# Nine 2x2 groups with seven products in the second MLP's down-projection

## The reference

```python
up = causal_dwconv(h @ w_up[l], conv_w[l], conv_b[l])        # 2 x 5632 channels, 3 taps
y = (gelu(up[..., :5632], approximate=True) * up[..., 5632:]) @ w_down[l]   # 5632 -> 2048
x = x + rms_norm_2(y, post_ffn_g[l])
```

## Time and profile before

| | us |
|---|---|
| median of the three runs | 2084.43 |
| the profiled execution | 2085.97 |
| its span, first to last instruction | 2084.2 |
| TensorE busy | 2075.1 |
| VectorE busy | 1332.8 |
| ScalarE busy | 1110.3 |
| GpSimd busy | 117.6 |

### The profile page before, as it was taken

How to read it: one execution, slowest core, us unless ns; L and a number is a source line. 1 busy time by engine, 2 the same in 40 slices (tenths; PEclk the granted TensorE clock), 3 DMA queues, 4 the chain that set the end, 5 groups by cost and what they waited for, 6 DMA issues and landing times.

```text
span 2084.2 us, 23926 instructions
## 1 busy us (share of the span) xinstructions
PE 2075.1 (100%) x9259; PEld 1720.2 (83%) x9259; DVE 1332.8 (64%) x1471; ACT 1110.3 (53%) x1344; POOL 117.6 (6%) x66
## 2 busy tenths in 40 slices
PE   9999999999999999999999999999999999999998
PEld 8888888888888878888888888888888888888887
DVE  6546555666884579666876655566767754576665
ACT  7555554555554455455555544456555534555553
POOL 3000000000000000000002000000111100021110
PEclk9999999999999999999999999999999999999999
DMA  8687666778757776778778777677787766778763
GB/s 294 196 258 230 190 187 222 256 220 260 223 187 223 225 238 210 223 222 232 241 254 242 215 252 229 193 212 233 232 262 223 237 196 192 234 235 257 244 214 120
DMA packets 291906, 469.49 MB, mean 225 GB/s; under 512 B 18512, under 2 KB 82128, under 8 KB 291280
## 3 DMA queue, kind: packets, MB, share of 16 engines
q1 hardware_dynamic: 290928, 463.46, 72.3%
q10 hardware_dynamic: 864, 4.49, 0.6%
HBM read 432.75 MB, written 35.13 MB: 224 GB/s over the span
## 4 chain that ended last, share of the span: by engine, by line
PE 95%; DMA 2%; DVE 1%; ACT 1%; SPq 0%; issue 0%; POOL 0%; ACTq 0%; DVEq 0%; POOLq 0%
PE ps L1714 95%; DMA T<-passed_strip 1%; DMA passed_strip<-T 1%; DVE Wl L1335 0%; SPq L1036 0%; DVE T L1428 0%; ACT Wh L1111 0%; PE ps L1717 0%; ACT hid L1214 0%; ACT T L1171 0%; ACT T L1179 0%; DVE hid L1493 0%; SPq L1057 0%; ACT T L1269 0%; DVE QK L1608 0%
## 5 line engine op out<-in xcount | busy, mean ns | idle before, releaser
L1335 DVE TENSOR_TENSOR Wl<-raw,Wh 128x1024 fp32r<-128x1024 f32 x743 | 921.3, 1259 | 590.5 <-ACT Wh L1111 586.3
L1714 PE MATMUL ps<-Wh,aHL 128*128 128x512 f32 x3712 | 1148.9, 390 | 0.5 <-ACT aHL L1139 0.4
L1111 ACT ACTIVATE Wh<-raw 128x1024 fp32r<-128x1024 f32 x743 | 772.2, 1056 | 585.6 <-PE ps L1714 562.1
L1714 PEld LDWEIGHTS ps<-Wh,aHL 128*128 128x128 f32 x3712 | 697.1, 188 | 146.0 <-issue 1.4
L1714 PE MATMUL ps<-Wl,aHL 128*128 128x512 f32 x1856 | 722.3, 389 | 0.0
L1714 PE MATMUL ps<-Wh,hid 128*128 128x512 f32 x1578 | 489.4, 389 | 1.4 <-DVE Wl L1335 1.4
L1714 PEld LDWEIGHTS ps<-Wl,aHL 128*128 128x128 f32 x1856 | 348.6, 188 | 71.8
L1714 PEld LDWEIGHTS ps<-Wh,hid 128*128 128x128 f32 x1578 | 296.2, 188 | 63.5 <-issue 1.8
L1714 PE MATMUL ps<-Wl,hid 128*128 128x512 f32 x789 | 306.9, 389 | 0.0
L1714 PEld LDWEIGHTS ps<-Wl,hid 128*128 128x128 f32 x789 | 148.1, 188 | 30.6
L1714 PE MATMUL ps<-Wh,oHL 128*128 128x512 f32 x512 | 158.9, 390 | 0.0
(11 more groups left out here) (190 smaller groups left out, 876.4 us busy)
## 6 DMA issues: line engine op xcount, KB each, us to landing
raw<-in_mlp_w_dram SPq DMA_DIRECT2D x256, 512.0 KB, 5.2
raw<-in_w_up_dram SPq DMA_DIRECT2D x176, 512.0 KB, 4.5
raw<-in_sb_w_qkv_dram SPq DMA_DIRECT2D x93, 512.0 KB, 5.3
raw<-in_w_down_dram SPq DMA_DIRECT2D x88, 512.0 KB, 4.4
raw<-in_w_in_dram SPq DMA_DIRECT2D x64, 512.0 KB, 4.9
passed_strip<-T SPq DMA_DIRECT2D x104, 256.0 KB, 4.3
T<-passed_strip SPq DMA_DIRECT2D x208, 128.0 KB, 4.8
raw<-in_sb_w_o_dram SPq DMA_DIRECT2D x32, 512.0 KB, 5.2
```

Source lines behind the costliest of these rows:

```text
L1111: e.activation(Wh[:, i % NW, c], src, ACT.Copy).then_inc(st["hi"][0], 1)
L1335: e.tensor_tensor(Wl[:, i % NW, c], src, Wh[:, i % NW, c].bitcast(F32), ALU.subtract).then_inc(st["lo"][0], 1)
L1714: return e.matmul(o, l, r, start=start, stop=stop, skip_group_check=True)
```

## The change

Three of the four pairs of `w_down_2` get three groups each, from the hidden blocks 0, 1 and 4 of their part; pair 4 stays as it was. The token sums of these blocks are made in the up-projection, after the first and the third gated pair of strips of each part (`MIXED_STRIPS`), from the gate's buffer `E`. The sums of part one go straight into `xn` (`fresh`), and `y_first` adds to it instead of copying.

With A for the plain slabs of a pair's first strip, B for those of its second and G for a group, TensorE's order is now:

- pair 1: A1 to A7, G1, B1 to B3, G2, B4 to B6, G3, B7, A8, A9, B8, B9
- pair 2: A1 to A4, G1, A5 to A7, G2, A8, B1, B2, G3, B3, B4, A9, B5 to B9
- pair 3: A1 to A5, G1, B1, B2, G2, B3, B4, G3, B5, A6, A7, B6, B7

```diff
-    def strip_pair(w, s4, ks, tail, mov, tiles, evacs, koff=0, sevens=(), fold=None):
+    def strip_pair(w, s4, ks, tail, mov, tiles, evacs, koff=0, sevens=(), fold=None, lead=None):
...
-        lead, gap = (4, 3) if tail else (2, 3 if len(plain) > 7 else 2)
-        rest = a[lead:n] + b[:n] if tail else a[lead:n - 1] + b[:2] + a[n - 1:] + b[2:]
+        lead, gap = (lead or 4, 3 if lead is None or len(plain) > 7 else 2) if tail else (lead or 2, 3 if len(plain) > 7 else 2)
+        rest = a[lead:n] + b[:n] if tail else a[lead:n - 1] + b[:lead] + a[n - 1:] + b[lead:]
...
+    MIXED_STRIPS = {0: (0, 2), 8: (2, 1)}
...
                     free["E"] = [lo]
+                    if t0 in MIXED_STRIPS:
+                        free["E"] = [lo, mix_tokens("hid2", "E", *MIXED_STRIPS[t0], [g])]
...
             i = strip_pair("w_down_2", s4, tuple(range(2 * at, 2 * (at + n))), 0 if s4 else 2, "hid2", hid_tiles,
                            [evac_y(c, s4), evac_y(c, s4 + 1)], koff=2 * at)
+                           sevens=(2 * at, 2 * at + 1, 2 * at + 4) if c == 0 or s4 == 0 else (),
+                           fold=fold_into("xn", s4, fresh=c == 0), lead=4 if s4 else 2 * n - 5)
...
-        hid2, = area(("hid2", [128, 24, 2 * TOK], F32R))
+        hid2, hidMix2 = area(("hid2", [128, 24, 2 * TOK], F32R), ("hidMix2", [128, 3, 4, TOK], F32R))
...
+                        if st["fresh"]:
+                            e.tensor_copy(x[:, 0, a], P[:, 0, :]).then_inc(m[1][0], 1)
+                            e.wait_ge(*m[0])
+                            e.tensor_tensor(x[:, 1, a], P[:, 2, :], wsum[:, 0, :], ALU.add).then_inc(m[2][0], 1)
...
+                    elif st["fresh"]:
+                        e.tensor_tensor(x[:, 0, b], P[:, 1, :], wsum[:, 0, :], ALU.subtract).then_inc(m[3][0], 1)
+                        e.wait_ge(*m[2])
+                        e.tensor_tensor(x[:, 1, b], P[:, 1, :], x[:, 1, a], ALU.subtract).then_inc(m[4][0], 1)
...
-                        e.tensor_copy(xn[:, t, cs], ps[st["set"]][:, t, :]).then_inc(st["done"][t][0], 1)
+                        if st["folded"]:
+                            e.tensor_tensor(xn[:, t, cs], xn[:, t, cs], ps[st["set"]][:, t, :], ALU.add).then_inc(st["done"][t][0], 1)
+                        else:
+                            e.tensor_copy(xn[:, t, cs], ps[st["set"]][:, t, :]).then_inc(st["done"][t][0], 1)
```

More of the change, by code:

```diff
@@ L149, in plan_program, with mix_tokens @@
     mixed_tokens = {}
-    def mix_tokens(mov, k, n, need):
+    def mix_tokens(mov, src, k, n, need):
         d = [done("token_mixed") for c in range(4)]
         hi, lo = done("mixed_hi"), done("mixed_lo")
-        step("mix_tokens", mov=mov, k=k, n=n, need=[*need, *free["sums"]], d=d, hi=hi)
+        step("mix_tokens", mov=mov, src=src, k=k, n=n, need=[*need, *free["sums"]], d=d, hi=hi)
         free["sums"] = [lo]
@@ L160, in mix_tokens, with fold_into @@
         return d[3]
-    def fold_into(s4):
+    def fold_into(to, s4, fresh=False):
         def f(sets, k):
             copied = done("fold_copied")
-            marks = [done("folded") for i in range(8)]
-            step("fold", s4=s4, k=k, sums_free=list(free["sums"]), copied=copied, marks=marks)
+            marks = [done("folded") for i in range(5 if fresh else 8)]
+            step("fold", to=to, s4=s4, k=k, sums_free=list(free["sums"]), copied=copied, marks=marks, fresh=fresh)
             def second():
-                step("fold_rest", s4=s4, marks=marks)
+                step("fold_rest", to=to, s4=s4, marks=marks, fresh=fresh)
                 free["sums"], free["set2"] = [marks[-1]], [marks[-1]]
@@ L414, in landed @@
                 if mixed and t0 < 8:
-                    free["T1"] = [lo, mix_tokens("hid1", t0 // 2, 2 if t0 == 0 else 1, [turned])]
+                    free["T1"] = [lo, mix_tokens("hid1", "T1", t0 // 2, 2 if t0 == 0 else 1, [turned])]
                 hid_tiles[t0:t0 + 4] = [lo] * 4
@@ L442, in plan_program @@
             i = strip_pair("mlp_w2", s4, tuple(range(2 * at, 2 * (at + n))), 0 if s4 else 2, "hid1", hid_tiles, evacs, koff=2 * at,
-                           sevens=() if c == 2 and s4 else tuple(range(2 * at, 2 * at + 3)), fold=fold_into(s4))
+                           sevens=() if c == 2 and s4 else tuple(range(2 * at, 2 * at + 3)), fold=fold_into("xN", s4))
             if c == 1 and s4 == 0:
@@ L688, in f @@
                 d = [done("y_kept") for t in range(2)]
-                step("y_first", s4=s4, set=s, mm=k, done=d)
+                step("y_first", s4=s4, set=s, mm=k, folded=st.pop(("fold", s4), None), done=d)
                 free[f"set{s}"] = [d[1]]
@@ L694, in f @@
                 g = done("y_gained") if s4 < 3 else done("y_gained_last")
-                kw = dict(t=t, s4=s4, set=s, mm=k[t], t0_free=list(free["T0"]), y=y, q=q, g=g, g_row=st["g_row"])
+                kw = dict(t=t, s4=s4, set=s, mm=k[t], t0_free=list(free["T0"]), y=y, q=q, g=g, g_row=st["g_row"],
+                          folded=st.get(("fold", s4)))
                 free["T0"] = [q]
@@ L959, in build @@
         square_buf = {"E": E4, "T1": T1[:, :, :], "QK1": mT[:, 8:12, :]}
-        mixes = {"hid1": hidMix1}
+        mixes = {"hid1": hidMix1, "hid2": hidMix2}
         movs = {"aHL": aHL, "oHL1": oHL1, "oHL2": oHL2, "hid1": hid1, "hid2": hid2}
@@ L1348, in vector_program @@
                     d, hi, lo = mixed_rows(st)
-                    src = T1[:, :, :].rearrange("p (k t) q -> p t k q", t=2)
+                    src = (T1[:, :, :] if st["src"] == "T1" else E4).rearrange("p (k t) q -> p t k q", t=2)
                     even, odd = src[:, 0, 0:st["n"], :], src[:, 1, 0:st["n"], :]
@@ L1364, in vector_program @@
                 elif k in ("fold", "fold_rest"):
+                    x = xN if st["to"] == "xN" else xn
                     a, b = [slice((st["s4"] + i) * STRIP, (st["s4"] + i + 1) * STRIP) for i in range(2)]
@@ L1369, in vector_program @@
                         e.tensor_tensor(wsum[:, 0, :], P[:, 0, :], wsum[:, 0, :], ALU.add).then_inc(m[0][0], 1)
[L1370 to L1373, removed]
+                        if st["fresh"]:
[3 more added lines that the diff above has]
+                        else:
+                            e.tensor_tensor(x[:, 0, a], x[:, 0, a], P[:, 0, :], ALU.add).then_inc(m[1][0], 1)
+                            e.wait_ge(*m[0])
+                            e.tensor_tensor(wsum[:, 1, :], P[:, 2, :], wsum[:, 0, :], ALU.add).then_inc(m[2][0], 1)
+                            e.tensor_tensor(wsum[:, 2, :], P[:, 1, :], wsum[:, 0, :], ALU.subtract).then_inc(m[3][0], 1)
+                    elif st["fresh"]:
+                        e.tensor_tensor(x[:, 0, b], P[:, 1, :], wsum[:, 0, :], ALU.subtract).then_inc(m[3][0], 1)
+                        e.wait_ge(*m[2])
+                        e.tensor_tensor(x[:, 1, b], P[:, 1, :], x[:, 1, a], ALU.subtract).then_inc(m[4][0], 1)
                     else:
@@ L1376, in vector_program @@
                         e.tensor_tensor(wsum[:, 0, :], P[:, 1, :], wsum[:, 1, :], ALU.subtract).then_inc(m[4][0], 1)
-                        e.tensor_tensor(xN[:, 1, a], xN[:, 1, a], wsum[:, 1, :], ALU.add).then_inc(m[5][0], 1)
-                        e.tensor_tensor(xN[:, 0, b], xN[:, 0, b], wsum[:, 2, :], ALU.add).then_inc(m[6][0], 1)
+                        e.tensor_tensor(x[:, 1, a], x[:, 1, a], wsum[:, 1, :], ALU.add).then_inc(m[5][0], 1)
+                        e.tensor_tensor(x[:, 0, b], x[:, 0, b], wsum[:, 2, :], ALU.add).then_inc(m[6][0], 1)
                         e.wait_ge(*m[4])
-                        e.tensor_tensor(xN[:, 1, b], xN[:, 1, b], wsum[:, 0, :], ALU.add).then_inc(m[7][0], 1)
+                        e.tensor_tensor(x[:, 1, b], x[:, 1, b], wsum[:, 0, :], ALU.add).then_inc(m[7][0], 1)
                 elif k == "rms":
@@ L1592, in vector_program @@
                 elif k == "y_first":
+                    if st["folded"]:
+                        e.wait_ge(*st["folded"])
                     for t in range(2):
```

2 lines of the change are left out of this document (1 added, 1 removed).

## The result

The changed kernel takes 2092.38 us (median of six runs, 2090.84 to 2093.55), beside 2084.55 us for the kernel before in the same sitting: 1.003 times as long, with a 95% interval of 1.0019 to 1.0041. It is slower, as forecast, by 7.8 us between the medians (0.38%, inside that interval) where the forecast had 5.0. The profiled execution took 2091.95 us, its span is 2089.9.

The account below looks back on a forecast made before the run. TensorE, busy 2075.1 of 2084.2 us, was taken as the bound: 2085.97 - 6.12 + 3.7 (pair 1) + 7.4 (pair 3) = 2091.0, less 1.54 to the median, 2089.4 us. The range leaving out 2 in 10: 2085.5 to 2092.5.

Parts of the forecast that it names:

- What goes: Nine groups take 21 matmuls for 24: 27 x 0.2267 = 6.12 us less on TensorE's path.
- Pair 2 and the token sums at nothing: Pair 2's groups cost nothing; token sums taken as 0, with 0 to 0.5 us for each two-block place.
- Pair 1, 3.7 us: In pair 1, s2 of G2 0.98 us late and B5 2.74 us late, together 3.7 us.
- Pair 3, 7.4 us: In pair 3, s2 0.57, s3 2.40, B3 0.46 and G3's s0 3.96 us late, together 7.4 us.
- Rival 3: The clock falls in pair 3's 3.96 us wait, costing 2.3 us more: 2091.7 us; chance 0.15.
- a granted clock below 1 near pair 3's G3: Listed among the signs that would show the forecast wrong; no size given.
- The gate waits for a break of VectorE: GpSimd's gate product starts only at a break in VectorE's row, then takes 2.26 us.
- The sum: 2085.97 - 6.12 + 3.7 + 7.4 = 2091.0 us, less 1.54 from profiled execution to median: 2089.4 us, 0.24% slower.
- the token sums' 1.54 us until the copy: With two blocks, the token sums cost VectorE 1.54 us until the copy starts, 428.48 to 430.06.
- Rival 2: The splits stay ahead, so only the 6.12 us count: 2078.3 us, faster; chance 0.08.

Follow-up runs that it names:

- pair 2 alone: The changed kernel with the groups of pairs 1 and 3 taken out, token sums still made in all four places: 2082.11 us.
- first filled kernel: The changed kernel with eight zero-weight matmuls run by TensorE in pair 3's wait before s3 of G2: 2091.36 us.
- the second: The changed kernel with eight zero-weight matmuls in pair 3's wait before s3 of G2 and fourteen before s0 of G3: 2092.42 us.
- the kernel with the chain later: The changed kernel with the last up strip's older taps, GpSimd gate product and halves placed later in pairs 1 and 3: 2088.23 us.
- the spread chain: The changed kernel with the last up strip's chain spread over the splits in pairs 1 and 3, and its gate product on VectorE: 2081.14 us.

## Why the prediction was right, and where its terms were off

- *What goes*: 27 matmuls, in pair 2 alone all of its 2.04 us. Right.
- *Pair 2 and the token sums at nothing*: right.
- *Pair 1, 3.7 us*: the two waits together are 1.17 + 2.53 = 3.70. That the sum is met so exactly is luck: the terms were 0.98 and 2.74. What was missing is the slow start behind a wait: the first matmul is 0.34 us before the next in place of 0.2267, and a few after it run a little long, 0.35 in all.
- *Pair 3, 7.4 us*: where the clock did not fall it is 7.57 in the first filled kernel and 8.52 in the second, whose strip landed later. In the profiled execution it was 9.09. Rival 3 came on top of the forecast, and twice: a granted clock below 1 near pair 3's G3, one of the prediction's own signs of being wrong, was there (0.57 from 2007 to 2011). The first fall cost nothing, since it ran out of the wait before s0 of G3 (2.35 us for the forecast's 3.96); the second, behind that wait, cost 1.7 where the rival had 2.3. The prediction had the clock at 0.15 and as one event. In these traces the lower level followed most of the waits of 2.0 to 4.7 us, in pair 1 and in the first MLP too, but not three of them (2.2, 2.4 and 3.8 us).
- *The gate waits for a break of VectorE*: right in every profile here; all gate products of the thirteen profiles, of whatever length, end 2.20 to 2.27 us after the end of VectorE's last instruction before the break. The Trainium skill (SBUF — State Buffer, "SBUF: two separate sides") lets the port pair that VectorE and GpSimd share go to whichever of their instructions starts first. The runs agree that the other one then stands for the whole of it (2.77 us for the fourth sum), but between VectorE's back-to-back instructions GpSimd never came first.
- *The sum*: taking off the 1.54 us between the profiled execution and the median was sound. Most of that distance was the wait of 1.4 us in the first MLP, a chance of one execution, and the kernel before came out at 2084.55 again. The forecast had the change at 4.98 us, and the medians differ by 7.83. Of the missing 2.85 us, 1.7 lie in pair 3, by the clock, and 0.35 in pair 1, by the slow starts. The remaining 0.8 are in no pair: 0.43 is that the profiled execution lies so much below its own median, and no trace places the rest. The median ended 0.1 us inside the upper end of the range, 2092.5.
- *A slip without weight*: the token sums' 1.54 us until the copy is 1.58 by the starts given for it, 428.48 and 430.06.
- *Rival 2 (the splits stay ahead)* named the place that decides, and the spread chain shows it: with the taps out of the way of the splits and the gate product in VectorE's own row, pair 1 has no wait at all.

## What to carry to other kernels

Work that is placed by a count of pieces moves in time when the pieces get shorter: look for what stands between the splits of the new pieces before counting the matmuls saved. GpSimd's product beside a busy VectorE cost twice here, first by waiting for a hole and then by making VectorE stand for its length; on this critical chain the same operation in VectorE's own row was cheaper (1.14 us for some 2.1). And where VectorE has no lead left, as in pair 3, the saved matmuls came back as waits (54.34 us with the groups and the chain spread, 54.40 without groups): such groups can be left out.

## What the runs showed that was not expected

- A hole of 0.12 us in VectorE's row, where an instruction waits for the result of the one before, was enough for GpSimd to get in, in both pairs of the kernel with the chain later: 2.08 and 2.03 us for VectorE.
- TensorE's granted clock went to 0.50 behind a wait of 2.4 us in one execution and stayed at 1.00 behind one of 3.77 us in another.
- The first matmul behind a wait is followed by the next after 0.34 us (0.30 at s0 of G3), where the pace is 0.2267.
